# Output projection of the later tokens: three products of split operands in place of one of raw operands

## The reference, cut to what matters

```
g = sigmoid(gate_logits)                      # 4 x 1024 per token
m = g[0]*(y0 @ w_branch[0]) + ... + g[3]*(y3 @ w_branch[3])
x = x + g1 * (m @ w_out)                      # output projection, 1024 x 1024
x = x + g2 * conv_ffn(modulate(rms_norm(x, norm2), sh2, sc2), w_up, ...)
```

## Time and profile before

| | us |
|---|---|
| median of 3 runs | 2585.21 (2583.32 to 2585.3) |
| the profiled execution: its own time | 2588.45 |
| its span, first to last instruction | 2586.6 |
| PE busy in the span | 2503.1 |
| PE busy on raw output products (L1270), both layers | 56.2 |

### The profile page before, as it was taken

How to read it: one execution, slowest core, us unless ns; L and a number is a source line. 1 busy time by engine, 2 the same in 40 slices (tenths; PEclk the granted TensorE clock), 3 DMA queues, 4 the chain that set the end, 5 groups by cost and what they waited for, 6 DMA issues and landing times.

```text
span 2586.6 us, 37764 instructions
## 1 busy us (share of the span) xinstructions
PE 2503.1 (97%) x15409; PEld 2089.5 (81%) x15409; DVE 1362.0 (53%) x1820; ACT 750.7 (29%) x1268; POOL 1495.5 (58%) x1375
## 2 busy tenths in 40 slices
PE   7999999999999999999999999999999999999998
PEld 4987988877778878888877889887777678888777
DVE  5622276453678776555574453337655788411341
ACT  5401333422456421111120123133522564111200
POOL 3533488423324527666679436448734456688896
PEclk9999999999999999999999999999999999999999
DMA  9524321314215625343433463212222246333231
GB/s 316 155 73 127 82 72 64 88 58 112 64 58 179 214 90 147 114 130 115 119 103 120 122 212 101 70 49 84 76 58 72 78 160 207 107 98 98 81 97 67
DMA packets 379633, 286.98 MB, mean 111 GB/s; under 512 B 10581, under 2 KB 339897, under 8 KB 378950
## 3 DMA queue, kind: packets, MB, share of 16 engines
q1 hardware_dynamic: 377296, 281.76, 36.5%
q10 hardware_dynamic: 1558, 2.72, 0.3%
q0 software_dynamic: 608, 0.09, 0.0%
HBM read 253.07 MB, written 29.36 MB: 109 GB/s over the span
## 4 chain that ended last, share of the span: by engine, by line
PE 80%; DVE 10%; POOL 4%; ACT 3%; issue 1%; DMA 1%; SPq 0%; DVEq 0%; ACTq 0%; POOLq 0%
PE ps L563 18%; PE ps L565 17%; PE ps L564 17%; PE ps L1334 3%; PE ps L791 3%; PE ps L613 2%; PE ps L615 2%; PE ps L614 2%; POOL w_lo L1500 2%; DVE ffl L2660 2%; ACT arena L1833 2%; PE ps L918 1%; PE ps L1270 1%; PE ps L822 1%; PE ps L859 1%
## 5 line engine op out<-in xcount | busy, mean ns | idle before, releaser
L1497 POOL TENSOR_TENSOR w_hi<-ring,tiny 128x512 fp32r<-128x512 f32 x480 | 542.9, 1131 | 919.6 <-PE ps L565 609.0
L1500 POOL TENSOR_TENSOR w_lo<-ring,w_hi 128x512 fp32r<-128x512 f32 (+1 forms) x568 | 805.5, 1421 | 82.4 <-ACT w_hi L1711 44.7
L563 PE MATMUL ps<-hh,w_hi 128*128 128x512 f32 (+1 forms) x2288 | 828.7, 362 | 8.5 <-DVE hl L2152 4.1
L565 PE MATMUL ps<-hh,w_lo 128*128 128x512 f32 (+1 forms) x2288 | 806.8, 353 | 0.0
L564 PE MATMUL ps<-hl,w_hi 128*128 128x512 f32 (+1 forms) x2288 | 806.7, 353 | 0.0
L563 PEld LDWEIGHTS ps<-hh,w_hi 128*128 128x128 f32 x2288 | 434.8, 190 | 104.5 <-issue 27.3
L565 PEld LDWEIGHTS ps<-hh,w_lo 128*128 128x128 f32 x2288 | 434.1, 190 | 60.8
L564 PEld LDWEIGHTS ps<-hl,w_hi 128*128 128x128 f32 x2288 | 435.4, 190 | 55.7 <-issue 0.5
L2005 ACT ACTIVATE arena<-ps,vec 128x768 f32<-128x768 f32 (+1 forms) x44 | 39.1, 888 | 423.8 <-PE ps L565 423.8
L1833 ACT ACTIVATE arena<-ps,tiny,vec 128x768 f32<-128x768 f32 (+1 forms) x120 | 108.7, 906 | 182.4 <-DVE tiny L2383 182.3
L2669 DVE SCALAR_TENSOR_TENSOR arena<-ps,vec,arena 128x511 f32<-128x511 f32 x66 | 43.6, 661 | 220.1 <-ACT arena L2005 219.3
(11 more groups left out here) (281 smaller groups left out, 3796.8 us busy)
## 6 DMA issues: line engine op xcount, KB each, us to landing
ring<-in_w_in SPq DMA_DIRECT2D x118, 512.0 KB, 4.1
ring<-in_w_mod SPq DMA_DIRECT2D x96, 512.0 KB, 3.9
ring<-in_w_up SPq DMA_DIRECT2D x88, 512.0 KB, 4.4
ring<-in_w_down SPq DMA_DIRECT2D x48, 512.0 KB, 3.6
ring<-in_w_out SPq DMA_DIRECT2D x32, 512.0 KB, 4.2
logits<-arena SPq DMA_DIRECT2D x32, 384.0 KB, 2.6
arena<-logits SPq DMA_DIRECT2D x32, 384.0 KB, 4.5
ring<-in_w_down SPq DMA_DIRECT2D x24, 384.0 KB, 3.1
```

Of the source, the lines that this page charges most:

```text
L563: pe.matmul(acc, wh[:, offset + k], hi[:, n, x:y], start=n == 0, stop=False)
L565: mm = pe.matmul(acc, wl[:, offset + k], hi[:, n, x:y], start=False, stop=n == whole - 1)
L1497: pool.tensor_tensor(wh[:, 0:count], w, one[:].unsqueeze(2).to_broadcast([P, count, P]), ALU.mult).then_inc(*up("w_lead", ("lead", key, j)))
L1500: pool.tensor_tensor(wl[:, 0:count], w, wh[:, 0:count].bitcast(F32), ALU.subtract).then_inc(*up("w_split", ("split", key, j)))
```

## The change

The later tokens' sums are no longer kept raw. `mh` and `ml` now hold all tokens of the layer, so ACT makes one high part of full width in place of two copies, and POOL and DVE make rests of full width. The `oraw` chunks count as split chunks: the projection of the `second` part is now `product` of 12 products a half, 24 a chunk. ACT makes the high parts of the `oraw` chunks 0 to 3 ahead of the norm `first`, those of 4 to 7 inside it behind k = 1, 3, 5 and 7, and those of up0 and up1 behind it. POOL makes the rests of all of these.

```diff
@@ led_by_act, is_split
-    return key[0] == "out" or (key[0] == "wb" and key[2] >= 2)
+    return key[0] in ("out", "oraw") or (key[0] == "wb" and key[2] >= 2) or (key[0] == "up" and key[2] < 2)
-    return key[0] not in ("mod", "msl", "slice", "dctx", "oraw")
+    return key[0] not in ("mod", "msl", "slice", "dctx")
@@ tensor
-                    pe.wait_ge(*at(("landed", key)))
-                    for k in range(KT):
-                        mm = pe.matmul(psum(key)[:, 0:z - y], raw(key)[:, k], m_late[:, k, y:z], start=k == 0, stop=k == KT - 1)
-                    mm.then_inc(*up("pe_raw", ("used", key), ("full", key)))
+                    for j in range(2):
+                        pe.wait_ge(*at(("split", key, j)))
+                        product(psum(key)[:, 0:z - y], key, j, mh, ml, y, z, first=KT // 2 * j).then_inc(
+                            *up("pe_half", ("half", key, j), *([("full", key)] if j else [])))
@@ gpsimd, rest_of_sum (and the same in vector, with 0:w for 0:y)
-                w = PARTS[l, 2]["first"][1]
+                w = W[l]
@@ scalar, norm_of
-            def norm_of(l, which, part, between={}):
+            def norm_of(l, which, part, between={}, leads={}):
...
+                    if k in leads:
+                        lead(leads[k])
@@ scalar, lead_of_sum
-                    y = PARTS[l, 2]["first"][1]
-                    act.activation(m_late[:, u, y:w], m_sum[:, u % 2, y:w], ACT.Copy)
-                    act.activation(mh[:, u, 0:y], m_sum[:, u % 2, 0:y], ACT.Copy).then_inc(*up("lead_ready", ("mh", l, u)))
+                    act.activation(mh[:, u, 0:w], m_sum[:, u % 2, 0:w], ACT.Copy).then_inc(*up("lead_ready", ("mh", l, u)))
@@ scalar, order
-                norm_of(l, 2, "first")
+                for u in range(KT // 2):
+                    lead(("oraw", l, u))
+                norm_of(l, 2, "first", leads={2 * n + 1: ("oraw", l, KT // 2 + n) for n in range(KT // 2)})
+                for c in range(2):
+                    lead(("up", l, c))
                 norm_of(l, 2, "second")
```

More of the change, by code:

```diff
@@ L424, in bass_hybrid_backbone @@
         mh = nc.alloc_sbuf_tensor_at("mh", [P, KT, T], F32R, offset=arena_at + 4 * 8 * T)
-        m_late = arena[:, 8 * T:16 * T].rearrange("p (k t) -> p k t", t=T)
         ml = nc.alloc_sbuf_tensor_at("ml", [P, KT, T], F32R, offset=arena_at + 4 * 16 * T)
@@ L2629, in rest_of_sum @@
                 def rest_of_sum(u):
-                    y = PARTS[l, 2]["first"][1]
                     dve.wait_ge(*at(("mh", l, u)))
-                    dve.tensor_tensor(ml[:, u, 0:y], m_sum[:, u % 2, 0:y], mh[:, u, 0:y].bitcast(F32), ALU.subtract).then_inc(
+                    dve.tensor_tensor(ml[:, u, 0:w], m_sum[:, u % 2, 0:w], mh[:, u, 0:w].bitcast(F32), ALU.subtract).then_inc(
                         *up("rest_ready", ("ml", l, 0, u)))
```

## The result

The changed kernel takes 2606.59 us (median, 2600.26 to 2609.29) against 2585.26 before: 21.3 us slower, a ratio of 1.0079 (95% interval 1.0066 to 1.0092). The forecast was slower by 19 us, 2604 in 2593 to 2612.

What follows compares the result with a forecast made beforehand. DVE's chain was taken to bound layer 0, with about a microsecond to spare in layer 1; PE's 8.8 us were not subtracted. Layer 0's 9.4 and layer 1's 9.8 make 19.2 us slower: 2604, range 2593 to 2612.

Steps and rivals of the forecast that it cites:

- The bound: In the changed stage, DVE's chain bounds layer 0 and has about a microsecond to spare in layer 1.
- The late root: Before the norm, ACT's leads of chunks 0 to 3 delay the root: +5.9 us in layer 0, +4.9 in layer 1.
- The norm: In the first part's norm, POOL's rests slow DVE instructions: +0.3 us in layer 0, +6.6 in layer 1.
- The residuals: Leftover rests meet DVE's second residuals: +3.2 us in layer 0; layer 1 -1.2, and -1.0 for squares not waiting.
- The rest: Elsewhere, POOL's wider rests of the sums: hidden in layer 0, +0.5 us in layer 1; other changes nothing.
- The sum: All terms of the stage: 9.4 us in layer 0 and 9.8 in layer 1, together 19.2 us slower.
- Rival 1: At chunk 4 of the raw ones, PE's saving counts: -8.8 us, 2576; chance 5%.
- Rival 2: Before and in the norm, the late root costs, the contention hardly: 10.6 us slower, 2596; chance 17%.
- Rival 3: Longer PE gaps in the stage cost clock, stretches at half speed: +3 to 5 us, 2608; chance 15%.
- Rival 4: At the root, a table switch costs its drain, root 1.4 us later in both layers: +2.8 us, 2607; chance 3%.
- Rival 5: The change doesn't do what it says; halves shared another way, stage keeps its length: 2585; chance 3%.

Runs made afterwards that it cites:

- half_raw: Kernel before, but PE makes only 4 of the 8 raw products of each chunk of the later tokens; 2583.52 us, ratio 0.9987.
- narrow_rests: Changed kernel, but POOL's rests of chunks 4 to 7, up0 and up1 have 16 columns instead of 512; 2588.77 us, ratio 1.0003 to the kernel before.
- last_rest_late: Changed kernel with only the rest of the sum u = 6 moved behind the split of the second out chunk; 2606.15 us, ratio 1.0086 to the kernel before.
- up_leads: Kernel before, raw products kept, but ACT makes the high parts of up0 and up1 behind the first part's norm; 2580.59 us, ratio 0.9988.
- wide_rest: Kernel before with POOL's rests of the sums at full width for u = 0 to 6; 2586.01 us, ratio 0.9999.
- root_early: Changed kernel, but ACT leads chunks 2 and 3 of the later tokens behind the root; 2600.18 us, ratio 1.0049 to the kernel before.

## Why the prediction was right, and where it wasn't

**The bound.** Right. half_raw takes 27 us of PE's work away for 3.4 us. I gave layer 1 "about a microsecond to spare"; with much less PE work 2.9 us came out of its stage. The root moves by 1.5 us when chunk 0 gets shorter (4.30 to 2.76), the norm gives that back (9.41 to 10.94), since POOL's splits now reach into it, and the residuals are 2.7 us shorter (18.06 to 15.40): the squares no longer wait for PE, and fewer of POOL's instructions meet them.

**The late root.** Predicted +5.9 and +4.9, measured +6.0 (4.93 to 10.95) and +4.25 (4.30 to 8.55). In layer 1 I let the squares meet a rest of POOL; PE took them without a wait. PE's own waits behind it cost nothing, but I had drawn them too large for layer 0: 4.9 us before chunk 4, and then 3.0 in two more, not 2 to 4 before each chunk.

**The norm.** Predicted +0.3 and +6.6, measured +0.20 and +6.63. The count is right as well as the sum: seven rests, in layer 1 each of them slows one instruction by 0.9 to 1.0 us, and in layer 0 six are slowed. narrow_rests shows the cause: 15.42 and 9.75 us with POOL's instructions cut short.

**The residuals.** Predicted +3.2 in layer 0 and -2.2 in layer 1, measured +3.26 and -2.34. The exact hit in layer 0 is partly luck. I took the residuals before as undisturbed, but their first squares took 0.99 us, slowed by POOL's last split from the norm. And six rests meet them, not five: against the 12.37 of narrow_rests they cost 3.8 us, 0.63 each as priced, and the kernel before already carried 0.55 of that. In layer 1 it is five rests, as I said; but the 14.6 us that I gave for the eight residuals is not what my own terms make (11.7 and 5 x 0.65 are 14.9). They take 14.4, since undisturbed they take 11.05 (narrow_rests) and not 11.7.

**The rest: the step that failed.** I put the wider rests of the sums at nothing in layer 0, "hidden in layer 0 under 8 branch sums with PE never idle". The cover was named too widely. All are hidden but the last of POOL's seven: it stands in front of the split of the second `out` chunk, for which PE waits, and it cost 2.2 us in the profiled execution (72.11 against 69.94; 69.92 in last_rest_late, where it stands behind that split). I had seen this wait in layer 1, where PE already stood idle, and didn't ask what margin layer 0 had at the same place. It came 1.3 us later than before, and took 1.36 us longer (2.66 against 1.30), where I took 0.5 for the width in layer 1. In layer 1 the sums grew by 1.1 us, not 0.5, but not where I said: PE's wait for POOL's weight rest is 1.3 us now, and the 2.31 of the earlier trace rows was no constant: up_leads and half_raw, with the sums as before, have 1.0 and 0.9. What is longer in all kernels with wide rests is PE's wait for DVE's sums at the first `out` chunk, 2.8 us or more where the kernels with narrow ones have at most 1.9.

**The sum.** Layer 0: 9.4 predicted, 11.7 measured. Layer 1: 9.8 and 9.2. The 2.2 us of layer 0 are what the sum lacked; an overestimate of 0.6 in layer 1 takes part of it back, 19.2 against 20.9 in the stages.

**The rivals.** Rival 1 (PE's saving counts) fell with half_raw and with the 4.89 us of PE idle at chunk 4, the place that it named. Rival 2 (the contention hardly costs) fell with the norm of layer 1. Rival 3 (gaps cost clock) happened in part, as the next section shows; it stretched PE where PE was waiting anyway. DVE's chain didn't get longer by it: its idle time from the first residual of the second part to the second reciprocal is 2.13 us in both layers, as in narrow_rests. Rival 4: the root starts 1.28 us behind the start of the table load plus 0.02 us (928.01 to 929.31). The load was on the path this time, and no drain of 1.4 us stands beside it; the figure in the Trainium skill (ScalarE: Activation LUTs, What ACT_TABLE_LOAD costs), 2.66 us for a switch, does not fit this place. Rival 5 fell with the 64 split products a layer in the profile.

**What stays open.** What the wide rest costs in an average execution (wide_rest's profile is of its longest), why ACT's last high part comes later in layer 0, and whether last_rest_late gains its 2.2 us in the total. The differences are of the size by which single executions of the kernel before scatter (2580.5 to 2591.6).

## What to carry to other kernels

Price a saving on the busiest engine only after the chain of waits of that very stage has been read: here PE was 97% busy, and half of its raw products could go for 3.4 us. When work moves to an engine that has idle time, look at what stands behind it in that engine's order, and at which instructions of its neighbours run at the same time: POOL's rests cost DVE more than PE saved. Of several parts of a change try the smallest alone: two leads more on ACT, without the split products, were some 3 us faster than the kernel before, where the whole change was 20 slower.

## What the runs showed of the hardware that I had not expected

**The clock behind PE's waits.** The windows after, layer 0 (length, busy PE, PEld, DVE, ACT, POOL; clock). PE is busy for 1.08 of 3.3 us while it waits for chunk 4, and the next 6.8 us are granted 0.50, the 1.2 GHz level; then full speed, 2.4 GHz, again.

```profile
932.00:935.30 3.30, 1.08 (x10) 0.88 (x8) 3.10 (x5) 0.89 (x2) 0.00 (x0) 1.00 0.11 32
935.30:942.10 6.80, 4.13 (x19) 4.16 (x20) 6.69 (x7) 4.16 (x8) 3.67 (x3) 0.50 0.23 70
```

The mean granted clock fell from 0.995 to 0.991 in the profiled executions. narrow_rests has a wait of 3.8 us at the same place and again 6.8 us at about half clock behind it (0.52), and loses nearly nothing in the total. Stretches at half clock also lie far from the change, at other places in each execution: the kernel before had three between 1650 and 1940 us that the changed one did not, and it takes 4.9 us longer between the two stages. The changed kernel in turn takes 2.5 us longer ahead of the first stage and behind the second. So the profiled spans differ by 18.5 us and the stages by 20.9.

**DVE pays for the length of a POOL instruction, one for one.** A DVE instruction of 256 columns with both operands in SBUF takes 0.48 us alone. Each 512-column rest of POOL that overlaps DVE's row of them makes one of them take 1.37 to 1.52 us: seven for seven rests in the changed kernel, nine for nine in root_early. Rests of 16 columns, 0.32 us long in the mean, leave it at 0.48 and 0.49. A residual with one operand in PSUM takes 0.48 us in all these kernels, and so does DVE's reciprocal keep its 1.75 us with a rest beside it.
